# Splitting the token operands of three gate and up products during the output projection

## The reference, cut to what matters

```
x  = x + concat(y_conv, y_mlstm) @ w_out          # output projection, 16 tiles of 128 rows of x
hn = rmsnorm(x) * norm2_g
x  = x + (silu(hn @ w_gate) * (hn @ w_up)) @ w_down
```

## Time and profile before

| | |
|---|---|
| median of 3 runs | 2513.78 us (2510.97 to 2527.22) |
| the profiled execution | 2525.42 us, its span 2523.5 us, mean granted clock 0.99 |
| busy share of the span | PE 98%, PEld 96%, DVE 71%, ACT 35%, POOL 1% |
| the output projection on PE | about 764 to 958 us |
| group 0 of gate and up | 958 to about 993 us, group 1 to about 1020 us |

### The profile page before, as it was taken

The page is one execution under the profiler, slowest core; times in us unless marked ns, Lnnn a source line. Parts: engine busy times, 40 slices in busy tenths (PEclk is TensorE's granted clock), DMA queues, the critical chain, the costliest instruction groups (busy, mean ns, idle before and its releaser), DMA issues.

```text
span 2523.5 us, 44736 instructions
## 1 busy us (share of the span) xinstructions
PE 2468.8 (98%) x17714; PEld 2410.7 (96%) x17714; DVE 1787.7 (71%) x2497; ACT 894.4 (35%) x1236; POOL 36.9 (1%) x59
## 2 busy tenths in 40 slices
PE   8999999999999998999999999999999899899998
PEld 7999999999999998999999999999999899899886
DVE  7576575575687668887777777877777966866435
ACT  5212222222233335344343433434444533544313
POOL 0000000000000000000000000000000000000100
PEclk9999999999999999999999999999999999999999
DMA  5333333333235665344343433434334645744722
GB/s 129 95 121 94 87 105 99 91 100 95 81 115 160 186 188 188 113 126 117 101 132 111 125 114 104 126 114 120 115 98 132 228 142 167 238 136 140 261 89 75
DMA packets 458924, 325.55 MB, mean 129 GB/s; under 512 B 14131, under 2 KB 429007, under 8 KB 456369
## 3 DMA queue, kind: packets, MB, share of 16 engines
q1 hardware_dynamic: 403704, 250.29, 33.7%
q10 hardware_dynamic: 51448, 58.42, 7.6%
q0 software_dynamic: 3584, 14.16, 1.5%
HBM read 264.49 MB, written 58.34 MB: 128 GB/s over the span
## 4 chain that ended last, share of the span: by engine, by line
PE 91%; DVE 5%; issue 1%; DMA 1%; ACT 1%; SPq 0%; DVEq 0%; ACTq 0%
PE ps L600 21%; PE ps L834 16%; PE ps L838 16%; PE ps L836 16%; PE ps L603 10%; PE ps L608 4%; PE ps L937 2%; PE ps L939 2%; PE ps L941 2%; DVE oplo L2216 1%; DVE gw_ring L2070 1%; DMA opraw<-hop 0%; PE ps L945 0%; DMA xtok<-in_x_sample_dram 0%; PE ps L946 0%
## 5 line engine op out<-in xcount | busy, mean ns | idle before, releaser
L834 PE MATMUL ps<-ophi,gw_ring 128*128 128x288 f32 x3360 | 999.8, 298 | 29.5 <-DVE cacc L2237 8.5
L836 PE MATMUL ps<-oplo,gw_ring 128*128 128x288 f32 x3360 | 995.0, 296 | 0.0
L838 PE MATMUL ps<-ophi,gw_ring 128*128 128x288 f32 x3360 | 993.2, 296 | 0.0
L834 PEld LDWEIGHTS ps<-ophi,gw_ring 128*128 128x128 f32 x3360 | 633.9, 189 | 33.9 <-DVE cacc L2237 9.2
L838 PEld LDWEIGHTS ps<-ophi,gw_ring 128*128 128x128 f32 x3360 | 636.6, 189 | 0.0
L836 PEld LDWEIGHTS ps<-oplo,gw_ring 128*128 128x128 f32 x3360 | 634.9, 189 | 0.1
L1002 ACT ACTIVATE whi<-wraw 128x512 fp32r<-128x512 f32 x256 | 160.7, 632 | 610.0 <-PE ps L603 466.2
L600 PE MATMUL ps<-xhi,whi 128*128 128x288 f32 x1536 | 334.0, 299 | 0.0
L600 PE MATMUL ps<-xlo,whi 128*128 128x288 f32 x1536 | 329.7, 296 | 0.0
L603 PE MATMUL ps<-xhi,wlo 128*128 128x288 f32 x1536 | 329.6, 296 | 0.0
L2070 DVE TENSOR_TENSOR gw_ring<-graw_a,gw_ring 128x1024 fp32r<-128x1024 f32 x200 | 244.7, 1224 | 119.2 <-ACT gw_ring L1249 118.7
(11 more groups left out here) (329 smaller groups left out, 2566.7 us busy)
## 6 DMA issues: line engine op xcount, KB each, us to landing
wraw<-in_w_in_dram SPq DMA_DIRECT2D x96, 512.0 KB, 3.8
graw_a<-in_w_ffn_gate_dram SPq DMA_DIRECT2D x59, 512.0 KB, 3.7
graw_a<-in_w_ffn_up_dram SPq DMA_DIRECT2D x59, 512.0 KB, 4.9
graw_a<-in_w_ffn_down_dram SPq DMA_DIRECT2D x42, 512.0 KB, 5.7
wraw<-in_w_out_dram SPq DMA_DIRECT2D x32, 512.0 KB, 3.9
opraw<-hop SPq DMA_DIRECT2D x14, 1152.0 KB, 10.5
graw_b<-in_w_ffn_gate_dram SPq DMA_DIRECT2D x29, 512.0 KB, 3.7
graw_b<-in_w_ffn_up_dram SPq DMA_DIRECT2D x29, 512.0 KB, 4.5
```

The lines of the kernel that those rows point to most:

```text
L834: pe.matmul(out, gw_ring[:, slot, 0, k, :], ophi[p][:, k, :], start=start and k == 0, stop=False, skip_group_check=True)
L836: pe.matmul(out, gw_ring[:, slot, 0, k, :], oplo[p][:, k, :], start=False, stop=False, skip_group_check=True)
L838: mm = pe.matmul(out, gw_ring[:, slot, 1, k, :], ophi[p][:, k, :], start=False, stop=k == GK - 1, skip_group_check=True)
```

## The change

The blocks for the last three products (4, 5, 6: `tsum[1]`, `xg[1,1]`, `tsum[2]`) are split in the output projection. In `pair_done` ACT copies them to high parts in a new buffer `tst` (576 and 288 columns), waits for its own copy (`x_hi`), and stores them in one transfer of 432 KB. DVE makes the low parts in place (`late_low`, two subtractions) in the odd tile of the next pair; ACT stores those in two transfers (`low_store`, 288 and 144 KB). `xg[:, 1]` of a pair now also waits until the low parts of the pair before have landed (`gw_in`), and that store is issued only just ahead, in the same tile. After the output projection SP loads two unsplit operands as before, then waits for the last low store, and loads high and low parts of the other three: eight transfers of 1008 KB in place of five. ACT and DVE split there only the eighth block of operands 4 to 6. `tst` lies where ring slot 2 will be, so ACT waits for the last high store before it writes product 2's weights.

```
+        tst = at("tst", [P, 3, HT], F32R, X0 + 16384)
...
-            for j in range(5):
+            for j in range(2):
                 sp.dma_start(opraw[j + 2][:, 0:GK - 1, :], opr[j][:, 0:GK - 1, :]).then_inc(tok_in[j], 16)
+            sp.wait_ge(gw_in, 32 * (GK - 1) + 16)
+            for j in range(3):
+                k = slice(0, GK - 1)
+                sp.dma_start(ophi[j + 4][:, k, :].bitcast(F32), opr_hi[LATE_ROW[j]][:, k, :]).then_inc(tok_in[j + 2], 16)
+                sp.dma_start(oplo[j + 4][:, k, :].bitcast(F32), opr_lo[LATE_ROW[j]][:, k, :]).then_inc(tok_in[j + 2], 16)
...
# PE, first_group
+                    if p < 4:
...
+                    else:
+                        pe.wait_ge(tok_in[p - 2], 80)
+                        pe.wait_ge(op_lo, p + 3)
+                        product(0, 0, p, bank, start)
...
# ACT, pair_done
-                act.dma_start(opr[2, :, k].rearrange("p k t -> p (k t)"), tsum[:, 1, :]).then_inc(tsum_st, 16)
-                act.dma_start(opr[4, :, k].rearrange("p k t -> p (k t)"), tsum[:, 2, :]).then_inc(tsum_st, 16)
                 act.dma_start(opr[1, :, k].rearrange("p k t -> p (k t)"), xg[:, 1, 0, :]).then_inc(tsum_st, 16)
-                act.dma_start(opr[3, :, k].rearrange("p k t -> p (k t)"), xg[:, 1, 1, :]).then_inc(tsum_st, 16)
+                if not (isinstance(m, int) and m == 0):
+                    act.wait_ge(tsum_st, m * 48)
+                act.activation(tst[:, 0:2, :], tsum[:, 1:3, :], ACT.Copy)
+                act.activation(tst[:, 2:3, :], xg[:, 1, 1:2, :], ACT.Copy).then_inc(x_hi, 1)
+                act.wait_ge(x_hi, m + (KT + 1))
+                act.dma_start(opr_hi[:, :, k].rearrange("q p k t -> p q (k t)"), tst[:].bitcast(F32)).then_inc(tsum_st, 16)
+
+            def low_store(m):
+
+                k = ds(m, 1)
+                act.wait_ge(x_lo, m + (KT + 1))
+                act.dma_start(opr_lo[0:2, :, k].rearrange("q p k t -> p q (k t)"), tsum[:, 1:3, :]).then_inc(gw_in, 16)
+                act.dma_start(opr_lo[2:3, :, k].rearrange("q p k t -> p q (k t)"), xg[:, 1, 1:2, :]).then_inc(gw_in, 16)
...
# ACT, out_tile, p == 1, ahead of the write of xg
-                        act.wait_ge(tsum_st, m * 80)
+                        act.wait_ge(tsum_st, m * 48)
+                        act.wait_ge(gw_in, m * 32 + 16)
...
-                out_tile(m, 1, lambda q: out_hi(m * 2 + 2, q), None, (m + 1, 0))
+                out_tile(m, 1, lambda q: out_hi(m * 2 + 2, q), lambda: low_store(m - 1), (m + 1, 0))
...
             def begin(q):
+                if q == 2:
+                    act.wait_ge(tsum_st, 48 * (GK - 1))
...
-            out_tile(KT // 2 - 1, 1, begin, last=True)
+            out_tile(KT // 2 - 1, 1, begin, lambda: low_store(GK - 2), last=True)
...
-            operand_hi(2)
...
-            operand_hi(3)
...
-            operand_hi(4)
...
# DVE, operand_low
+                pieces = [(last, GK, last_pair[j])]
+                if j < 2:
+                    pieces += [(0, 4, opraw[j + 2][:, 0:4, :]), (4, last, opraw[j + 2][:, 4:last, :])]
...
+            def late_low(m):
+
+                dve.wait_ge(x_hi, m + (KT + 1))
+                dve.wait_ge(t_step, m * 4 + 4)
+                tt(tsum[:, 1:3, :], tsum[:, 1:3, :], tst[:, 0:2, :].bitcast(F32), ALU.subtract)
+                tt(xg[:, 1, 1:2, :], xg[:, 1, 1:2, :], tst[:, 2:3, :].bitcast(F32), ALU.subtract).then_inc(x_lo, 1)
+
             def after_pair(m):
                 first_low(m)
                 second_low(m - 1)
+                late_low(m - 1)
```

More of the change, by code:

```diff
@@ L295, in hybrid_trunk_step @@
         x1_t = nc.dram_tensor("x1_t", [KT, P, T], F32, kind="Internal").ap()
-        opr = nc.dram_tensor("opr", [5, P, GK, HT], F32, kind="Internal").ap()
+        opr = nc.dram_tensor("opr", [2, P, GK, HT], F32, kind="Internal").ap()
+        opr_hi = nc.dram_tensor("opr_hi", [3, P, GK, HT], F32, kind="Internal").ap()
+        opr_lo = nc.dram_tensor("opr_lo", [3, P, GK, HT], F32, kind="Internal").ap()
+        LATE_ROW = (0, 2, 1)
         h_t = nc.dram_tensor("h_t", [FT - FS, P, T], F32, kind="Internal").ap()
@@ L484, in sum_load @@
                     else:
-                        sp.wait_ge(tsum_st, 80 * (GK - 1) + 16 * (d // 2))
+                        sp.wait_ge(tsum_st, 48 * (GK - 1) + 16 * (d // 2))
                 elif d >= PPC + 2:
@@ L495, in _ @@
             sp.wait_ge(w_used, 4 * I_FFN)
-            sp.wait_ge(tsum_st, 80 * (GK - 1))
-            for j in range(5):
+            sp.wait_ge(tsum_st, 48 * (GK - 1))
+            for j in range(2):
                 sp.dma_start(opraw[j + 2][:, 0:GK - 1, :], opr[j][:, 0:GK - 1, :]).then_inc(tok_in[j], 16)
+            sp.wait_ge(gw_in, 32 * (GK - 1) + 16)
[3 more added lines that the diff above has]
+                sp.dma_start(oplo[j + 4][:, k, :].bitcast(F32), opr_lo[LATE_ROW[j]][:, k, :]).then_inc(tok_in[j + 2], 16)
             sp.wait_ge(ss2_mm, 1)
@@ L890, in first_group @@
                         pe.wait_ge(ready, 1)
[L891 to L894, removed]
+                    if p < 4:
+                        pe.wait_ge(op_lo, 3 * (p - 2) + 2)
+                        product(0, 0, p, bank, start, (0, 4))
+                        pe.wait_ge(op_lo, 3 * (p - 2) + 3)
+                        product(0, 0, p, bank, start, (4, GK))
+                    else:
+                        pe.wait_ge(tok_in[p - 2], 80)
+                        pe.wait_ge(op_lo, p + 3)
+                        product(0, 0, p, bank, start)
                     if p == 2:
@@ L909, in down_group @@
                     else:
-                        before = 15 + 14 * (d // PPC) + 2 * p
+                        before = 9 + 14 * (d // PPC) + 2 * p
                         pe.wait_ge(op_lo, before + 1)
@@ L1312, in hidden_hi @@
             def hidden_hi(c, j):
-                act.wait_ge(d_in[j] if j < 2 else tok_in[j - 2], 16 * (c + 1) + (0 if j < 2 else 64))
+                act.wait_ge(d_in[j] if j < 2 else tok_in[j - 2], 16 * (c + 1) + (0 if j < 2 else 64 if j < 4 else 80))
                 for k0, k1 in ((0, 4), (4, GK)):
@@ L1991, in first_sum @@
                 if not (isinstance(m, int) and m == 0):
-                    dve.wait_ge(tsum_st, m * 80)
+                    dve.wait_ge(tsum_st, m * 48)
+                    dve.wait_ge(gw_in, m * 32 + 16)
                     dve.wait_ge(t1_lo, m)
@@ L2076, in operand_low @@
                 last = GK - 1
-                for n, (k0, k1, src) in enumerate(((last, GK, last_pair[j]), (0, 4, opraw[j + 2][:, 0:4, :]),
-                                                   (4, last, opraw[j + 2][:, 4:last, :]))):
-                    dve.wait_ge(op_hi, 3 * j + n + 1)
+                pieces = [(last, GK, last_pair[j])]
+                if j < 2:
+                    pieces += [(0, 4, opraw[j + 2][:, 0:4, :]), (4, last, opraw[j + 2][:, 4:last, :])]
+                for n, (k0, k1, src) in enumerate(pieces):
+                    dve.wait_ge(op_hi, (3 * j if j < 2 else j + 4) + n + 1)
                     tt(oplo[j + 2][:, k0:k1, :], src, ophi[j + 2][:, k0:k1, :].bitcast(F32),
@@ L2214, in hidden_low @@
                 for n, (k0, k1) in enumerate(((0, 4), (4, GK))):
-                    dve.wait_ge(op_hi, 15 + 14 * c + 2 * j + n + 1)
+                    dve.wait_ge(op_hi, 9 + 14 * c + 2 * j + n + 1)
                     tt(oplo[j][:, k0:k1, :], opraw[j][:, k0:k1, :], ophi[j][:, k0:k1, :].bitcast(F32),
```

## The result

The changed kernel is slower: its median over 22 runs is 2526.28 us (2515.73 to 2532.35), that of the kernel before, in the same rounds, 2520.32 us (2510.97 to 2527.67). The ratio is 1.0025 with a 95% interval of 1.0015 to 1.0035, 6.3 us (3.8 to 8.8); a second measurement gave 1.0022 (1.0012 to 1.0033). The kernel before timed against itself gave 1.0001 (0.9990 to 1.0012), so a tenth of a per cent is what such a comparison resolves. The forecast of 2517.7 us, +3.9 on 2513.8, had the right sign against the three runs it was reckoned on; over 22 runs the kernel before takes 2520.3 itself, and the change is clear of noise where "same" was forecast. The measured median lies just inside the stated range, 0.2 us under its upper end, and that end came from the scatter of three runs, not from the sum.

The account below looks back on a forecast made before the run. PE, busy 98% of the span, was taken as the bound, so only its holes could give time back; +6.1 - 2.24 = +3.9 us on 2513.8 gave 2517.7 us, range 2507.5 to 2526.5.

Parts of the forecast that it names:

- The chain: Handover after output projection: third weight block lands 983.3, five DVE steps, product 6 at 989.18, norm, 1003.15; program end moves equally.
- -2.24 us: DVE in `operand_low(4)`, behind the weight block's arrival: two large subtractions go, saving 2.24 us on the critical path.
- I take none: SP's queue after the output projection: pause for the last low store, up to 2 us, counted as zero.
- I take 2.1 us: Group 1's weight loads: three blocks at 2.1 us each, 6.3 us behind the last operand load, landing at 989.4.
- The sum: Product 6's start and all behind it: +6.1 - 2.24 = +3.9 us, with +1.6 and +5.9 as other ends.
- 2513.8 + 3.9: Whole program: the earlier runs' median of 2513.8 us plus the forecast difference of 3.9, giving 2517.7 us.
- about 1%, 25 us, is what a measurement can tell from no change: Verdict on the whole program's time: faster 0.01, same 0.96, slower 0.03.
- Rival A: Handover: the weight block is not late, landing by 982, and the split saves 3.5 to 5 us; chance 0.17.
- The two cancel: Handover: weight block lands between 983 and 987, the change giving -2.2 to +1.4 us; chance 0.17.
- Rival B: Output projection stalls on the odd tile's low store, +12 us if it lands after 10 us; chance 0.06.
- Both are earlier than product 6: hidden.: Handover: `x1` and `xg` 1.1 to 4.5 us later, product 5 ending 986.2 or 989.6, before product 6's 993.1: no cost.
- PE's hole before product 6 grows to about 7 us: PE in the handover: hole grows from 3.2 to about 7 us, 3.5 if the first two holes take their worst.

Follow-up runs that it names:

- the high parts alone: Changed kernel with the early store, low-part loads of token operands 4 to 6 left out, PE multiplying high parts instead; handover 42.9 us, ratio to before 1.0006.
- the store early: Changed kernel with the last pair's low parts stored ahead of product 2's weight copy instead of behind it; handover 45.9 us, ratio to before 1.0004.
- Three more loads: Kernel before, with SP loading three of the five unsplit operands twice, eight transfers ahead of group 1's weights; handover 48.3 us, ratio to before 1.0022.
- the loads-held run: Changed kernel with the early store, SP holding its six loads until DVE's last sum of the last pair; handover 49.0 us, ratio to before 1.0022.
- store early and sum later: Changed kernel with the early store, group 1's first weight sum moved behind product 6's steps and the norm's reciprocals; ratio to before 0.9984.
- the fastest kernel: Changed kernel with the early store, product 6's steps and both norm halves ahead of group 1's first weight sum; ratio to before 0.9972.
- one operand split early: Changed kernel with the early store, only product 6's operand split in the output projection, six loads ahead of the weights; handover 44.0 us, ratio to before 0.9999.

## Why the prediction was right in its mechanism and wrong in its verdict

- **The chain.** Right: the third weight block, DVE's steps, product 6, the norm, the end. In the profile after, the 4.58 us at product 6's start reappear unchanged behind the last hole, and when the experiments move the block by 3.2 to 3.7 us, the handover moves by the same to 0.1. Not exact is that the end of the program moves by as much: behind the handover the stretch to 1240 took 241.4 to 244.0 us in the kernels with this order, by the clock that PE was granted there.
- **"-2.24 us".** Right: 5.25 to 3.01 us between block and `upper_up`, and -2.1 of handover with the high parts alone.
- **"I take none"** (SP's pause for the last low store, the term that was put at nothing). This step failed. I gave the store the 3.2 us of the earlier trace rows, though the row of a store issued into full queues, 8.0 us, was there and I had named it; it took 8.1. SP issued the six loads at S + 8.6, and the eighth landed at S + 27.6 in place of the predicted 25.0, against 23.9 with the store early. From block to block the two kernels are 3.7 us apart, more than the 2 that I kept for it.
- **"I take 2.1 us" for each weight block.** This failed too, the other way: blocks queued behind running loads followed at 1.4 to 1.6 us, three within 4.5 us. The 2.1 of the earlier trace rows are of a queue that had been empty. Three more loads cost 3.3 us by themselves, where my expectation for them was 4.9.
- **The sum** of +3.9 was thus near the measured +4.6 by luck, two errors that nearly cancel: the eighth load came 2.7 us later than reckoned, the three weight blocks behind it took 2.0 less. The experiments' own terms add up to the same: 3.3 (three loads) + 3.7 (the pause) - 2.24 = 4.8.
- **"2513.8 + 3.9" and "about 1%, 25 us, is what a measurement can tell from no change".** The step that made the verdict wrong. The median of three runs was 6.5 us low, so that the time given lay under that of the unchanged kernel; and the measurement resolves 0.1%, with 7 to 35 runs of each kernel in place of three. A shift of 4 to 6 us, worked out as such, had to be forecast as slower, not as the same.
- **Rival A** (the split saves what it should) did not happen: the block landed at S + 32.1, past the 982 (S + 24) that it needed. **"The two cancel"** is what the early store gives, +0.9 of handover. **Rival B** did not happen: 120.00 of 120.00 us again, and the odd tile's low store landed in 2.4 us at the median; DVE kept 0.96 of its 1.85 us.
- **"Both are earlier than product 6: hidden."** Right: `xg` came at 960.05, S + 8.7 against 4.4 before, and the loads-held run shows that this costs the handover nothing. The ratio's 5.5 to 6.3 us are 1 to 2 more than the handover's 4.6; the intervals hold both, and whether anything lies behind the difference stays open.
- **"PE's hole before product 6 grows to about 7 us".** It grew to 4.96. The sum started at S + 32.1 (31.3 forecast) and product 6 followed 3.5 us behind it, as forecast; but product 5 ended 2.8 us later than before, through the late `xg`. The prediction had this as its worst case, with 3.6 us and a hole of 3.5.

## What to carry to other kernels

Work moved off an engine saves time only if what that engine waits for next doesn't come later for it: splitting ahead of time turned five loads into eight, on the queue in front of the very transfer that the engine waited for. A store that a load queue waits for belongs ahead of large loads, not beside them: the low store landed 2.2 us after its issue ahead of them and 8.1 beside them, and the one line moved gave back 3.7 of the 4.6 us. And a wait for a transfer, once it is there, is a place to put work that needs nothing of it (here the norm): filling it, with the early store, took the kernel 0.28% below the one before (not shown is what the same order gives without the split).

## What the runs showed of the hardware

The same stretch of the output projection took 192.25 us in twelve profiles and 187.48 in two (before with three more loads; store early and sum later), each with the clock granted at 1.00 of 2.4 GHz and PE full. Windows of the kernel before and of the one with more loads, 50 us each, with the columns of the earlier trace rows:

```profile
805.00:855.00 50.00, 50.00 (x377) 50.00 (x376) 34.62 (x56) 16.42 (x28) 0.00 (x0) 1.00 0.61 186
```

```profile
800.00:850.00 50.00, 50.00 (x387) 50.00 (x386) 35.95 (x59) 16.75 (x28) 0.00 (x0) 1.00 0.64 193
```

377 against 387 matmuls: 0.133 and 0.129 us from one to the next at the same granted clock. No edit explains it, and what does stays open. In these two cases PE finishes the output projection earlier against DVE, whose chain sets the first holes of the handover: they come 0.5 us later from S with more loads than before, and 0.9 later with store early and sum later than with the store early alone. Lengths that this chain sets read too long by as much; the block's landing, which the queue sets from S on, doesn't.

The work ahead of the output projection, untouched too, took 516.2 to 524.0 us in the 14 profiles, from the last hole near 242 us to the first of the output projection, and here the granted clock goes with it. The longest, in the kernel before, and the shortest, in the fastest kernel:

```profile
241.89:765.89 524.00, 522.35 (x3754) 506.62 (x3755) 334.06 (x621) 124.80 (x199) 22.07 (x33) 0.98 0.33 96
242.27:758.46 516.19, 514.61 (x3754) 500.27 (x3755) 333.63 (x620) 124.29 (x199) 21.68 (x33) 1.00 0.34 97
```

The matmuls are as many, and the idle time is alike (1.65 and 1.58 us); PE's busy time differs by the 7.7 us, at a clock of 0.98 against 1.00. Single runs scatter in the same way: of the 23 runs of the kernel before that were timed beside the last experiments, the fastest, 2514.89 us, had a mean granted clock of 0.994, the slowest, 2527.42 us, one of 0.989. So the ends of spans don't compare, but stretches within the handover do.

After a hole of 2.60 us the kernel before ran at a granted clock of 0.64 for 4.75 us (24 matmuls, 1003.15 to 1007.90): part of this time at the lower level, 1.2 GHz, part at the upper. After one of 1.48 us the kernel with three more loads kept 1.00:

```profile
996.27:1001.02 4.75, 4.75 (x35) 4.75 (x36) 4.51 (x7) 3.40 (x5) 0.00 (x0) 1.00 0.38 110
```

That is 35 matmuls in place of 24, and accounts for its stretch to 1240 us being only 2.0 us longer where its handover is 3.3 longer. The length of the hole doesn't decide it alone, though. The kernels without the low parts and with one operand split early both have a hole of 2.95 us here, one of 0.93 us 6.4 us ahead of its end, and went on like this:

```profile
992.67:997.42 4.75, 4.75 (x20) 4.75 (x21) 4.50 (x7) 2.13 (x3) 0.00 (x0) 0.50 0.38 110
```

```profile
998.90:1003.65 4.75, 4.75 (x35) 4.75 (x36) 4.50 (x7) 3.39 (x5) 0.00 (x0) 1.00 0.39 110
```

The first ran at the lower level throughout, the second at the upper, and the stretches behind the handover are 2.2 us apart (244.0 and 241.8). What the clock costs is thus part of what a change in the handover is worth, and one profile of a kernel doesn't fix it.
